# PEER routing: gathers compared and multiplied in PSUM, both tiles' scores copied out early, gates spread from block 43

## What is computed

```python
def peer_ffn(hn, wq, subkeys, down, up):
    q = (xt @ wq).reshape(N, H, 2, PEER_DKEY // 2)
    s = jnp.einsum('nhpd,hpkd->nhpk', q, subkeys).astype(jnp.float32)
    s_half, i_half = lax.top_k(s, K)
    cand_s = (s_half[:, :, 0, :, None] + s_half[:, :, 1, None, :]).reshape(N, H, K * K)
    cand_i = (i_half[:, :, 0, :, None] * PEER_NKEYS + i_half[:, :, 1, None, :]).reshape(N, H, K * K)
    top_s, pos = lax.top_k(cand_s, K)
    eidx = jnp.take_along_axis(cand_i, pos, axis=-1)
    gate = jax.nn.softmax(top_s, axis=-1)
    ...
        act = jax.nn.gelu(jnp.einsum('cd,chkd->chk', xc, down[ec])) * gc
        return jnp.einsum('chk,chkd->cd', act, up[ec])
```

## Time and profile before

| | |
|---|---|
| median of 3 runs (lowest, highest) | 2612.46 us (2609.99, 2615.14) |
| the profiled execution | 2610.01 us, its span 2608.2 us |
| TensorE busy | 2398.2 us, 92% of the span |
| VectorE, ScalarE, GpSimd busy | 1724.1, 1346.5, 759.7 us |
| HBM read | 379.74 MB, 146 GB/s over the span |
| first PEER layer, down blocks | 422 to 836 us |
| second PEER layer, down blocks | 1814 to 2228 us |

### The profile page before, as it was taken

One profiled execution on the slowest core, in us unless ns is written; L12 is line 12 of the kernel. 1 busy time (PEld: TensorE's weight loads), 2 busy tenths in 40 slices (PEclk: granted clock), 3 DMA queues, 4 the chain that ended last, 5 costly groups with the idle time before them and its releaser, 6 DMA issues.

```text
span 2608.2 us, 39087 instructions
## 1 busy us (share of the span) xinstructions
PE 2398.2 (92%) x15394; PEld 2158.3 (83%) x15394; DVE 1724.1 (66%) x3220; ACT 1346.5 (52%) x2462; POOL 759.7 (29%) x358
## 2 busy tenths in 40 slices
PE   6878998999999999998878888799999999999998
PEld 5876888999999888886757877598999999888886
DVE  4564457977887555555777285366996788555555
ACT  3344344458887444443443344234447888444443
POOL 3000003887775000000000043200897777000000
PEclk8888899999999999998889988899999999999999
DMA  5322334555555666663422343235555555666663
GB/s 165 128 89 65 99 103 150 164 172 159 166 157 169 187 189 189 186 188 104 129 81 87 132 122 114 65 107 175 164 169 170 160 162 161 181 186 188 191 187 121
DMA packets 108285, 383.35 MB, mean 147 GB/s; under 512 B 12975, under 2 KB 15840, under 8 KB 107528
## 3 DMA queue, kind: packets, MB, share of 16 engines
q1 hardware_dynamic: 108104, 380.86, 47.7%
HBM read 379.74 MB, written 1.06 MB: 146 GB/s over the span
## 4 chain that ended last, share of the span: by engine, by line
PE 75%; DVE 15%; ACT 4%; POOL 2%; DMA 2%; issue 1%; SPq 0%; DVEq 0%; ACTq 0%; POOLq 0%
PE psum L370 21%; PE psum L372 21%; PE psum L371 21%; PE psum L2019 2%; POOL weight_parts L349 2%; PE psum L402 1%; DVE weight_parts L343 1%; ACT weight_parts L338 1%; PE psum L2682 1%; PE psum L607 1%; PE psum L2452 1%; DVE peer_experts L1906 1%; PE psum L1457 1%; DVE peer_experts L1905 1%; PE psum L1018 1%
## 5 line engine op out<-in xcount | busy, mean ns | idle before, releaser
L349 POOL TENSOR_TENSOR weight_parts<-weight_ring,weight_parts 128x1024 fp32r<-128x1024 f32 x276 | 697.5, 2539 | 538.8 <-ACT weight_parts L338 538.3
L370 PE MATMUL psum<-acts_high,weight_parts 128*128 128x256 f32 x2768 | 809.1, 292 | 46.3 <-DVE weight_parts L343 19.6
L338 ACT ACTIVATE weight_parts<-weight_ring 128x1024 fp32r<-128x1024 f32 x681 | 717.2, 1054 | 160.7 <-PE psum L372 62.4
L371 PE MATMUL psum<-acts_low,weight_parts 128*128 128x256 f32 x2768 | 793.3, 287 | 0.0
L372 PE MATMUL psum<-acts_high,weight_parts 128*128 128x256 f32 x2768 | 793.1, 287 | 0.0
L343 DVE TENSOR_TENSOR weight_parts<-weight_ring,weight_parts 128x1024 fp32r<-128x1024 f32 x405 | 497.0, 1228 | 314.7 <-ACT weight_parts L338 314.1
L370 PEld LDWEIGHTS psum<-acts_high,weight_parts 128*128 128x128 f32 x2768 | 538.9, 195 | 62.2 <-DVE weight_parts L343 21.5
L371 PEld LDWEIGHTS psum<-acts_low,weight_parts 128*128 128x128 f32 x2768 | 539.7, 195 | 2.8 <-issue 1.7
L372 PEld LDWEIGHTS psum<-acts_high,weight_parts 128*128 128x128 f32 x2768 | 539.3, 195 | 0.0
L370 PE MATMUL psum<-weight_parts,peer_coef 128*128 128x512 f32 x1024 | 405.7, 396 | 4.0 <-issue 3.9
L371 PE MATMUL psum<-weight_parts,peer_coef 128*128 128x512 f32 x1024 | 405.7, 396 | 0.0
(11 more groups left out here) (427 smaller groups left out, 3146.0 us busy)
## 6 DMA issues: line engine op xcount, KB each, us to landing
weight_ring<-in_peer_down SPq DMA_DIRECT2D x128, 512.0 KB, 3.6
weight_ring<-in_peer_up SPq DMA_DIRECT2D x128, 512.0 KB, 3.8
weight_ring<-in_peer_u SPq DMA_DIRECT2D x128, 512.0 KB, 3.6
weight_ring<-in_peer_v SPq DMA_DIRECT2D x128, 512.0 KB, 3.5
weight_ring<-in_w_in SPq DMA_DIRECT2D x88, 512.0 KB, 3.7
weight_ring<-in_w_out SPq DMA_DIRECT2D x16, 512.0 KB, 3.5
weight_ring<-in_peer_w_q SPq DMA_DIRECT2D x16, 512.0 KB, 3.7
weight_ring<-in_w_in_v SPq DMA_DIRECT2D x10, 512.0 KB, 4.0
```

The costliest lines, as they stand in the source:

```text
L338: q.e.activation(self.high, self.ring, ACT.Copy).then_inc(*self.rounded.once())
L349: q.e.tensor_tensor(self.low, self.ring, self.high.bitcast(F32), ALU.subtract).then_inc(*self.unit.ready.once())
L370: q.e.matmul(out, sh, mh, start=first, stop=False)
L371: q.e.matmul(out, sh, ml, start=False, stop=False)
```

## The change

1. `Routing` has two buffers of scores, one for each tile. The copy of tile 1's scores waits only for its own products, and each tile's ranking for its own copy.
2. The result of the comparison and of the multiplication (`eq`, 128 x 2048) lies in PSUM, banks 0 to 3, and the 4-bit positions (`part`) and the ramp in bank 7. The comparison now has one operand in SBUF (`partf`) and one in PSUM (the ramp), the multiplication one in PSUM and one in SBUF (`idxf`); the reduction reads PSUM. Before the first of them VectorE waits for both tiles' scores to have left banks 0 to 3 and for the ramp's copy.
3. The shifted scores and their exponentials (`gates`) lie in bank 6 for tile 0 and in bank 3 for tile 1 until the last multiplication.
4. Every reduction is followed by a wait for its end (`settle`).
5. `places = {3: tile 0, 5: tile 1, 39: both, 41: both}`, the ramp is copied ahead of the routing, and `first = 43`: the 64 groups are spread over 83 blocks in place of 77.

The number of instructions on TensorE, VectorE, ScalarE and GpSimd that compute is unchanged but for the gating of six more blocks in `Hidden`. SP's list is the same.

ScalarE at the start of the first PEER layer, before: the split of units 0 and 1, the copy of tile 0's scores, the split of unit 2.

```diff
--- before.py
+++ after.py
@@ -1825,8 +1825,13 @@
         self.turned, self.kept = c.mark("route_turned"), c.mark("route_pairs_kept")
         for b in range(4):
             c.bank_free[b] = (self.scores_kept,)
-        self.scores_free, self.res, self.zs = r.scores_free, r.res[i], r.zs[i]
-        r.scores_free, r.kept, r.scores_kept = (self.ranked,), self.kept, self.scores_kept
+        self.scores, self.res, self.zs = r.scores[i], r.res[i], r.zs[i]
+        self.eq = c.bank(0, 4).rearrange("p (h a b) -> p h a b", h=PEER_H, a=TOPK)
+        self.gates = c.bank((6, 3)[i])[:, 0:P].rearrange("p (h k) -> p h k", h=PEER_H)
+        small = c.bank(7).rearrange("p (x h k) -> p x h k", x=4, h=PEER_H)
+        self.part = small[:, 1, :, :].bitcast(U32)
+        self.iota16 = over(over(c.bank(7)[:, 0:TOPK], TOPK, 1), PEER_H, 1)
+        r.kept, r.scores_kept = self.kept, self.scores_kept
 
     def tensor(self, q):
         c, r = self.c, self.r
@@ -1852,17 +1857,17 @@
 
     def scalar(self, q):
         c, r = self.c, self.r
-        q.wait_ge(self.scored, *self.scores_free)
+        q.wait_ge(self.scored)
         if r.half_dim == 64:
             for a in range(2):
-                last = q.e.activation(r.scores[:, :, a, :], c.bank(2 * a, 2).rearrange("p (h n) -> p h n", h=PEER_H),
+                last = q.e.activation(self.scores[:, :, a, :], c.bank(2 * a, 2).rearrange("p (h n) -> p h n", h=PEER_H),
                                       ACT.Copy)
         else:
-            last = q.e.activation(r.scores, c.bank(0, 4).rearrange("p (h a n) -> p h a n", h=PEER_H, a=2), ACT.Copy)
+            last = q.e.activation(self.scores, c.bank(0, 4).rearrange("p (h a n) -> p h a n", h=PEER_H, a=2), ACT.Copy)
         last.then_inc(*self.scores_kept.once())
         yield
         q.wait_ge(self.shifted)
-        q.e.activation(self.res[:, 2, :, :], self.res[:, 2, :, :], ACT.Exp).then_inc(*self.powers.once())
+        q.e.activation(self.gates, self.gates, ACT.Exp).then_inc(*self.powers.once())
 
     def top16(self, q, vals, idx, src):
 
@@ -1888,7 +1893,7 @@
         q.wait_ge(self.scores_kept)
         last = self.top16(q, [r.vals[:, hd, a, :] for hd in heads for a in range(2)],
                           [r.idx[:, hd, a, :] for hd in heads for a in range(2)],
-                          [r.scores[:, hd, a, :] for hd in heads for a in range(2)])
+                          [self.scores[:, hd, a, :] for hd in heads for a in range(2)])
         last.then_inc(*self.ranked.once())
         q.wait_ge(self.ranked)
         q.e.tensor_copy(r.idxf, r.idx)
@@ -1898,20 +1903,21 @@
                                           [r.cand[:, hd, :, :].rearrange("p a b -> p (a b)") for hd in heads]))
         for a in range(2):
             if a == 0:
-                settle(c, q, "vector", q.e.tensor_scalar(r.part, r.pos, 4, None, ALU.logical_shift_right))
+                settle(c, q, "vector", q.e.tensor_scalar(self.part, r.pos, 4, None, ALU.logical_shift_right))
             else:
-                settle(c, q, "vector", q.e.tensor_scalar(r.part, r.pos, 15, None, ALU.bitwise_and))
-            settle(c, q, "vector", q.e.tensor_copy(r.partf, r.part))
-            settle(c, q, "vector", q.e.tensor_tensor(r.eq, over(r.partf, TOPK, 3), r.iota16, ALU.is_equal))
-            settle(c, q, "vector", q.e.tensor_tensor(r.eq, r.eq, over(r.idxf[:, :, a, :], TOPK, 2), ALU.mult))
-            q.e.tensor_reduce(self.res[:, a, :, :], r.eq, AX, ALU.add)
-        q.e.tensor_tensor(self.res[:, 2, :, :], r.top, over(r.top[:, :, 0], TOPK, 2), ALU.subtract).then_inc(
+                settle(c, q, "vector", q.e.tensor_scalar(self.part, r.pos, 15, None, ALU.bitwise_and))
+            settle(c, q, "vector", q.e.tensor_copy(r.partf, self.part))
+            q.wait_ge(r.scores_kept, r.iota_copied)
+            settle(c, q, "vector", q.e.tensor_tensor(self.eq, over(r.partf, TOPK, 3), self.iota16, ALU.is_equal))
+            settle(c, q, "vector", q.e.tensor_tensor(self.eq, self.eq, over(r.idxf[:, :, a, :], TOPK, 2), ALU.mult))
+            settle(c, q, "vector", q.e.tensor_reduce(self.res[:, a, :, :], self.eq, AX, ALU.add))
+        q.e.tensor_tensor(self.gates, r.top, over(r.top[:, :, 0], TOPK, 2), ALU.subtract).then_inc(
             *self.shifted.once())
         yield
         q.wait_ge(self.powers)
-        settle(c, q, "vector", q.e.tensor_reduce(self.zs, self.res[:, 2, :, :], AX, ALU.add))
+        settle(c, q, "vector", q.e.tensor_reduce(self.zs, self.gates, AX, ALU.add))
         settle(c, q, "vector", q.e.reciprocal(self.zs, self.zs))
-        q.e.tensor_tensor(self.res[:, 2, :, :], self.res[:, 2, :, :], over(self.zs, TOPK, 2), ALU.mult).then_inc(
+        q.e.tensor_tensor(self.res[:, 2, :, :], self.gates, over(self.zs, TOPK, 2), ALU.mult).then_inc(
             *self.weighed.once())
         yield
         tile = slice(P * self.i, P * self.i + P)
@@ -1928,7 +1934,6 @@
     def __init__(self, c, area, half_dim, q, sk, queries, pairs, gates_high, gates_low):
         self.half_dim, self.q, self.sk, self.queries, self.pairs = half_dim, q, sk, list(queries), pairs
         self.gates_high, self.gates_low = gates_high, gates_low
-        self.scores_free = ()
         at = [0]
 
         def cut(*shape):
@@ -1938,19 +1943,16 @@
             view = area[:, at[0] - n:at[0]]
             return view.rearrange(f"p ({' '.join(names)}) -> p {' '.join(names)}", **dict(zip(names, shape)))
 
-        self.scores = cut(PEER_H, 2, NKEYS)
+        self.scores = [cut(PEER_H, 2, NKEYS) for _ in range(NT)]
         self.cand = cut(PEER_H, TOPK, TOPK)
-        self.eq = cut(PEER_H, TOPK, TOPK)
         self.vals = cut(PEER_H, 2, TOPK)
         self.idx = cut(PEER_H, 2, TOPK).bitcast(U32)
         self.idxf = cut(PEER_H, 2, TOPK)
         self.top = cut(PEER_H, TOPK)
         self.pos = cut(PEER_H, TOPK).bitcast(U32)
-        self.part = cut(PEER_H, TOPK).bitcast(U32)
         self.partf = cut(PEER_H, TOPK)
         self.res = [cut(3, PEER_H, TOPK) for _ in range(NT)]
         self.zs = [cut(PEER_H) for _ in range(NT)]
-        self.iota16 = over(over(c.iota[:, 0:TOPK], TOPK, 1), PEER_H, 1)
 
 
 class CopyIota(Step):
@@ -2198,10 +2200,12 @@
         late_channels(c, [wq[n] for n in range(n_q)], gained, lambda n: Late(qs[:, n, :], 1.0, c), norm)
         c.flush(down[0], down[1])
         r = Routing(c, area[:, n_q * (P + T):], half_dim, qs, sk, [c.last_kept, sk_came], x.pairs, x.gates_high, x.gates_low)
+        x.iota_copied = r.iota_copied = c.plan(CopyIota(c)).copied
         routes = [Route(c, r, i) for i in range(NT)]
-        for i in range(NT):
-            c.bank_free[i] = (routes[i].kept,)
-        places = {2: routes[0:1], 14: routes[1:2], 44: routes, 47: routes}
+        for i in range(4):
+            c.bank_free[i] = (routes[1].kept,)
+        c.bank_free[6] = (routes[1].kept,)
+        places = {3: routes[0:1], 5: routes[1:2], 39: routes, 41: routes}
         x.there, x.gated, x.stored, x.routed = 0, 0, None, r.kept
         c.rotation = [4, 5]
         c.low_by = "pool"
@@ -2209,8 +2213,7 @@
             x.first = c.sb(name + "_first_keys", [P, 2, GROUP, P], inner, F32R)
             x.second = c.sb(name + "_second_keys", [P, 2, GROUP, 2, P], inner, F32R)
             x.hot_free, x.low_made, x.copy_free = [(), ()], None, None
-            x.iota_copied = c.plan(CopyIota(c)).copied
-            n_groups, used, finished, first = T // GROUP, 0, 0, 49
+            n_groups, used, finished, first = T // GROUP, 0, 0, 43
             onehots = []
             for n in range(NKEYS):
                 for route in places.get(n, ()):
```

## The result

| | before | after |
|---|---|---|
| median of 4 runs (lowest, highest) | 2612.17 us (2609.99, 2615.14) | 2592.93 us (2586.85, 2596.18) |
| ratio, 95% interval | | 0.9923 (0.990 to 0.9946) |
| the profiled execution, its span | 2610.01, 2608.2 us | 2596.18, 2594.4 us |

The change makes the kernel 19.2 us faster, where 12.3 us were forecast: 2600.2 us, with a range of 2595 to 2607. The sign, the mechanism and the places were right, and three terms of the sum were off, all to the same side.

The account below looks back on a forecast made before the run. TensorE, busy 2398 of 2608 us, was taken as the bound, so only its idle time could pay. -12.6 - 1.9 - 0.5 + 1.0 + 1.7 = -12.3 us took the median of 2612.5 to 2600.2 us, range 2595 to 2607.

Parts of the forecast that it names:

- Comparison, multiplication, position and cast: VectorE's ranking: one PSUM operand each ends turn-taking with GpSimd; tile 64.8 to 54.4 us, returning 12.6 us of TensorE waits.
- The candidates' sum stays: VectorE's sum with both inputs in SBUF still holds GpSimd up; four sums at 0.25 us, 1.0 us stays.
- Block 0 ahead of the scores: Start of both PEER layers: block 0 fills TensorE's wait before tile 0's scores; -1.9 us first layer, -0.5 second.
- Exponentials at 39: ScalarE's queue, 39 instead of 44: new deadline for the ranking; stalls of 1.1 and 0.6 us, +1.7 (0 to 12).
- Tile 1's copy: ScalarE's copy of tile 1's scores at 5 instead of 14: its wait stays hidden, costing nothing.
- the gates from 43: Spreading 64 groups over 83 blocks: no gain for TensorE, cost nothing; 5 us were the cover gone.
- D: Rival, whole kernel: everything fits, no stall left, 2597.5 us, down to 2595; chance below 2597 0.08.
- A: Rival: ranking misses its exponentials deadline, 8 to 9 us more, 2609; chance 0.17 in part, 0.1 in full or C.
- B: Rival: PSUM on both sides keeps comparison and multiplication at 4.4 us, TensorE stops 18 us twice, 2633 us; chance 0.05.
- C: Rival: GpSimd's delay comes from the landing of weights, only the start is won, 2610 us; chance 0.1 with A in full.

Follow-up runs that it names:

- The stops made on purpose: Changed kernel with GpSimd computing the low part of some units twice over, VectorE's work unchanged: 2610.77 us, ratio 1.0001.
- the last two kernels: Changed kernel with first up weighing planned ahead of the last two down blocks: 2586.18 us; the same plus one candidates' sum operand in PSUM: 2586.05 us.
- all in SBUF: Changed kernel's new places and gates from 43, but comparison, multiplication, positions, ramp and gates in SBUF as before: 2627.22 us, ratio 1.0067.
- ramp in SBUF: Changed kernel with only the comparison's ramp read from SBUF, its result still in PSUM: 2608.0 us, ratio 0.999.
- scores first: Changed kernel with the tiles' scores at 2 and 4 in place of 3 and 5, tile 0's ahead of block 0: 2589.82 us, ratio 0.992.

## Why the prediction missed

The account, in stretches of the first trace of each: forecast -12.3, measured -11.15 - 8.15 = -19.3, missing 7.0 us.

**Comparison, multiplication, position and cast: durations right, the return too small. This is the step that failed.** Forecast 2.30, 2.30, 0.26 to 0.28 us; measured 2.30, 2.30, 0.29. (The 16 ns that the prediction takes for a PSUM input are something else: both instructions of 697 and 681 ns in the earlier trace rows read PSUM, and only the first writes to it. It changed nothing.) The ranking of a tile went from 64.8 to 54.1 and 53.2 us (431.18 to 485.3, and on to 538.6), against 54.4 forecast, so two tiles were 107.4 in place of 108.8. What failed is that the prediction took the idle time listed by the waits, 12.6 us, for all that TensorE loses. Before's timeline of TensorE at the stop of 555.23:

```profile
553.58 0.28 PE L371 MATMUL psum<-acts_low,weight_parts 128*128 128x256 f32 x1
553.70 0.28 PE L372 MATMUL psum<-acts_high,weight_parts 128*128 128x256 f32 x1
555.23 0.38 PE L370 MATMUL psum<-acts_high,weight_parts 128*128 128x256 f32 x1 [1.25 <-POOL weight_parts L349]
555.46 0.28 PE L371 MATMUL psum<-acts_low,weight_parts 128*128 128x256 f32 x1
```

The matmul at 553.70 is shown until 553.98, but the next would have started at 553.82. From start to start the stop is 1.53 in place of 0.12, and the second matmul comes 0.23 after the first in place of 0.12: 1.52 us lost for 1.25 listed. Added up this way, the fourteen stops of before cost 8.8 + 7.5 = 16.3 us, and one of 0.07 us at 452.05, which the list leaves out, costs 0.3: 16.6 us and not 12.6. **4.0 us of the miss.** The stops made on purpose show a surplus of the same size, 0.23 us each in layer 2, with VectorE's operands as in the changed kernel.

**The candidates' sum stays, 1.0.** Right in size, by luck: the forecast had four stops of 0.25 us, and one came, in layer 1, listed with 0.7 us (the forecast's pieces were at most 0.6) and 1.0 from start to start; none in layer 2. The kernel with that sum in PSUM removed it and gave back 0.9 us.

**Block 0 ahead of the scores: 1.9 + 0.5 forecast, 3.0 + 0.9 measured** (from the last product of queries to the start of block 1, 9.98 us before and 7.02 after; in layer 2, 7.35 and 6.48). The order was right; the forecast took the scores' 3.40 us as their length. This window of the kernel before is those 32 products:

```profile
422.40:425.80 3.40, 3.32 (x32) 3.21 (x32) 0.22 (x2) 0.00 (x0) 0.00 (x0) 0.57 0.79 263
```

The clock was granted at 0.57 of full, after the wait of 3.40 us. With block 0 in that place TensorE waits 1.70 us, the granted clock stays at 1.00 and the products take 2.06. **1.4 us of the miss**, 1.1 of it in layer 1: the products that stand behind a wait were priced at the speed that they had there (1.3 us), while they start 0.3 us later than forecast (5.0 us after the last product of queries in place of 4.7). The rest is the stop of 0.52 us in layer 2, which costs 0.8 from start to start.

**Exponentials at 39: +1.7 forecast, 0 measured. 1.7 us of the miss.** The mechanism is right, as 36 in place of 39 shows, and so is the slack of nearly nothing. Two parts were off by 1.0 and 1.4 us, on the same side. The ranking started 9.2 us after the last product of queries (431.18 against 422.0) and not 10.2, since the scores were faster; and it was 1.4 us shorter. It ended at 538.6, or 116.6 after that product; the forecast had 119.0 against a deadline of 117.9. The transposes, moved to 41, also stand on TensorE ahead of the block that needs the late part (541.86 to 542.43), and give it another 0.6 us, which the forecast left out; without them the part would have been 0.5 us late.

**Tile 1's copy and the gates from 43: nothing, and nothing measured.**

4.0 + 1.4 + 1.7 = 7.1, against the 7.0 us that are missing. The 1.5 us by which layer 2's `up` stretch is shorter stood nowhere in the forecast, and no run shows that they belong to the change. Of the rivals, D ("everything fits") was the case that came. Its price, 2597.5 and at best 2595, took all listed waits as gone, so it had the same fault, and with it the low end of the range. A and B did not come here, but the kernel with the new places and all operands in SBUF shows the stop that both describe, 16 us slower than before (2627, where B had 2633). C is excluded: with every place and every transfer as before, the operands brought 15.8 us.

## What to carry to other kernels

Price a stop of a pipelined engine from start to start of its instructions, not by the idle time that a list of waits shows, and look at the granted clock (the share of its full clock that TensorE is given) right behind a wait before taking a duration from there. Where VectorE and GpSimd work side by side, count the SBUF inputs of each long VectorE instruction: in this kernel one operand moved to PSUM, a 16-element ramp, decided whether the other engine was held up. A step moved earlier has a deadline; compute it for the engine whose queue it blocks, and move it no further than the work ahead of it has become shorter.

## What the runs showed of the hardware

- An instruction of VectorE with two SBUF inputs and one of GpSimd wait for each other's whole length, even if VectorE writes to PSUM (4.19 us for 2.29). With one input in PSUM neither waits: 2.30 and 2.40 us.
- PSUM as an operand cost VectorE's long two-input instructions next to nothing here: 2.30 against 2.29 us for 2048 elements, and 2.28 either way for the candidates' sum. Position and cast of 128 elements, with one input, took 0.29 us with a side in PSUM, and 0.23 with both sides in SBUF where nothing held them up (before, 464.99 and 465.25). The Trainium skill (VectorE: DVE Perf Modes, "The TRN2 errata") gives 62 cycles more for a PSUM source, about 65 ns by estimate; the trace doesn't show them in the two-input instructions.
- The granted clock fell to 0.50 in or right behind waits of 3.40 us (before the scores), 8.9 us (exponentials at 36) and 2.37 us (split twice), and the matmuls behind them ran at 1.2 GHz, those of 128 x 256 at 0.21 in place of 0.12 us. In the kernel before none of the stops listed with 1.2 to 1.3 us did that, nor did the one of 1.70 us in the changed kernel.
- At the turn from down to `up`, idle for 1.93 us in every trace but those of the last two kernels, it sometimes falls and sometimes not. In the changed kernel's first trace it did: the window from 831 to 834 us has a granted clock of 0.51, and eight matmuls of 128 x 512 take 0.43 in place of 0.235 us, 1.5 us in all; in its second trace the same stretch runs at 1.00.

```profile
831.00:834.00 3.00, 3.00 (x9) 2.37 (x8) 1.23 (x1) 0.26 (x1) 0.00 (x0) 0.51 0.28 109
```

```profile
825.00:828.00 3.00, 3.00 (x14) 2.44 (x13) 1.23 (x2) 0.62 (x3) 0.00 (x0) 1.00 0.30 89
```

In layer 2 it fell in all three traces of the kernel before and in none of the changed one, though both wait 1.93 us there. But it fell there in four of the eight variants with that wait too (all in SBUF, ramp in SBUF, scores first, split twice), so this may be chance. Over both layers it fell at 12 of 28 such turns, and at none of the four that no longer wait. What decides it is open; no run here tells it.
